# A two-layer hybrid diffusion step on one core: next layer's modulation loaded and multiplied inside the attention, and expert routing from first lists

## The chip, the cores and the metric

One NeuronCore of a Trainium2 chip runs the whole program in one launch. The metric is the device time of one execution in microseconds (us).

## The reference, cut to what matters

640 tokens (512 latent, 128 context) of width 1024 pass through two layers. All weights are float32.

```
mod  = silu(c) @ w_ada[l] + b_ada[l]          # 1024 -> 6 x 1024: shift1, scale1, gate1, shift2, scale2, gate2
h    = rms_norm(x) * (1 + scale1) + shift1
proj = h @ w_in                               # attention (8 heads, 2 kv heads), chunk MLP, convolution
x    = x + gate1 * (concat(rms_norm(attn), rms_norm(sgu), rms_norm(conv)) @ w_out)
h2   = rms_norm(x) * (1 + scale2) + shift2
group = argmax(h2 @ rg);  top-2 of the 4 experts of that group, by h2 @ re
x    = x + gate2 * sum over 2 experts of gate * ((silu(h2 @ w1) * (h2 @ w3)) @ w2)
```

The first third of `mod` (shift1, scale1) of layer 1 depends on `c` alone, so it can be computed at any time in layer 0. The experts see their tokens as blocks of 128 rows: each of 16 experts has one first block, and there may be further ones (up to 26 in all).

## The kernel before

Each engine runs its own program in order and waits on semaphores; nothing is scheduled at run time. TensorE (PE) gets float32 accuracy from pairs: ScalarE (ACT) copies a weight unit of 128x2048 (1 MB) from `raw` to `wH` in a rounded type, VectorE (DVE) writes the remainder to `wL`, and three matmuls use them. So a unit is free again in `raw` when DVE's half of the split is done.

Weights are loaded by the queue of SyncE (SP). `STREAM` lists the 1 MB units in order: `("w", l, n)` are units of `w_in` (n under 8) and `w_out` (8 to 11), `("ada", l, n)` those of `w_ada` (8 for each third `q` of the modulation), which PE reads straight from `raw` in `ada_mm`. Unit i goes to slot i mod 4 of `raw`, and SP waits before each load until the unit four places ahead of it has been used (`unit_used`). SP works through the list in order, so a load whose slot is free still stands behind one whose slot is not.

In the attention of a layer PE, DVE and ACT walk over steps u = 0 to 43 (five token tiles of eight heads, and four steps to drain). In step u PE computes the scores of head u, transposes the probabilities of step u-2, and every other step multiplies them with the values. DVE takes the row maximum (L1284), ACT the exponential (L880). Into the steps are woven: the 16 `ada` units of this layer (`ADA_AT`, steps 2 to 29), and from step 31 on the splits of units 8 and 9 in quarters of 128x512 (`QUARTER_AT`; `quarter_hi` on ACT, L744, `quarter_lo` on DVE, L1157). Then come the merged transposes, two halves of the output projection, h2 and the router.

Layer 1's first eight `ada` units stand at the end of layer 0's list: PE takes two between the halves of the projection and six among the router's steps (`ada_next`), and DVE adds the bias (`piece_add`) after the routing. In layer 0 the splits of the first expert's w1 and w3 (`m_split(0, 0)` and `m_split(1, 0)`) come after the routing too; in layer 1 they come on ACT among the copies of the router, and on DVE between `normalised(4)` and the routing.

The routing is a chain of small DVE operations over 128 partitions: ranks of the logits (twice: groups, then the experts of the chosen group), choice, counts by matmul, ranks of tokens within experts, a one-hot of these (`one_r`, L1420), and lists by ten matmuls (L1888); from them `idxs` (L1438), after which GpSimd (POOL) gathers rows of h2 for the first two blocks (L650). PE transposes them (L1898), ACT copies (`x_hi`, L979), DVE subtracts (`x_lo`, L1475), and `w13` starts (L1566 to L1568). `ctl` holds the number of blocks, `slot` the rows that tokens find their results in.

## Time and profile before

| | |
|---|---|
| runs, median (lowest to highest) | 1110.79 us (1108.39 to 1112.57), 3 runs |
| the profiled execution | 1111.54 us, of which the span is 1109.7 |
| busy share | PE 89%, DVE 60%, ACT 53%, POOL 22% |
| mean granted clock of TensorE | 0.951 |
| mean DMA rate | 224 GB/s; above 400 in the experts' stages |

### The profile page before, as it was taken

The numbers are of one execution on the slowest core, as the hardware profiler recorded it, in microseconds if no ns is written. First come the engines' busy times: TensorE is split into PE (matmuls) and PEld (weight loads), VectorE is DVE, ScalarE is ACT, GpSimd is POOL, SyncE is SP. The second block draws the span as 40 slices with busy tenths as digits, with TensorE's granted clock in tenths as the row PEclk, the third lists the DMA queues.
The fourth block names the chain that finished last, engine by engine and source line by source line (L and its number), as shares of the span: only waits on it lengthen the run. The fifth ranks groups of instructions, "written<-read, shape, count | busy, mean of one in ns | idle before, by whom it ended". The sixth has DMA issues, their size and how long they took to land.

```text
span 1109.7 us, 15792 instructions
## 1 busy us (share of the span) xinstructions
PE 987.5 (89%) x5588; PEld 759.7 (68%) x5588; DVE 668.7 (60%) x970; ACT 587.1 (53%) x929; POOL 247.5 (22%) x304
## 2 busy tenths in 40 slices
PE   4899989986998699998989999899789739999984
PEld 2688865765874588887757887467568637888861
DVE  0359125655276799988444831455625659999936
ACT  4452235655222598887267222565623418988822
POOL 3034015211131122230411500620203212222031
PEclk9899999999998799999999999899889959999998
DMA  9695227553156899996771321565313448999944
GB/s 319 235 276 205 76 62 273 194 183 130 34 214 249 333 387 401 417 401 260 297 209 40 111 79 39 200 242 200 115 57 133 150 167 329 408 417 411 366 154 173
DMA packets 89091, 248.16 MB, mean 224 GB/s; under 512 B 25773, under 2 KB 30381, under 8 KB 79817
## 3 DMA queue, kind: packets, MB, share of 16 engines
q1 hardware_dynamic: 75960, 209.54, 50.9%
q0 software_dynamic: 11632, 32.60, 8.5%
q10 hardware_dynamic: 1440, 5.24, 1.2%
q8 instruction: 36, 0.59, 0.2%
q14 instruction: 23, 0.18, 0.0%
HBM read 220.82 MB, written 30.21 MB: 226 GB/s over the span
## 4 chain that ended last, share of the span: by engine, by line
PE 68%; DVE 9%; DMA 9%; ACT 7%; issue 4%; SPq 1%; POOL 0%; ACTq 0%; DVEq 0%; POOLq 0%
PE ps L1559 12%; PE ps L1561 12%; PE ps L1560 12%; DMA pool<-in_moe_w 6%; PE ps L1566 4%; PE ps L1568 4%; PE ps L1567 4%; PE ps L1577 4%; PE ps L1749 3%; PE ps L1764 3%; PE ps L1959 2%; PE ps L1738 2%; DVE wL L1358 2%; ACT wH L938 2%; PE ps L1898 2%
## 5 line engine op out<-in xcount | busy, mean ns | idle before, releaser
L1559 PE MATMUL ps<-wH,actH 128*128 128x512 f32 x608 | 248.6, 409 | 10.0 <-DVE actL L1487 5.2
L1561 PE MATMUL ps<-wH,actL 128*128 128x512 f32 x608 | 240.9, 396 | 0.0
L1560 PE MATMUL ps<-wL,actH 128*128 128x512 f32 x608 | 240.1, 395 | 0.0
L1358 DVE TENSOR_TENSOR wL<-raw,wH 128x2048 fp32r<-128x2048 f32 x64 | 146.2, 2285 | 14.1 <-ACT wH L938 13.6
L1559 PEld LDWEIGHTS ps<-wH,actH 128*128 128x128 f32 x608 | 116.5, 192 | 38.4 <-issue 9.1
L1561 PEld LDWEIGHTS ps<-wH,actL 128*128 128x128 f32 x608 | 116.0, 191 | 26.0
L1560 PEld LDWEIGHTS ps<-wL,actH 128*128 128x128 f32 x608 | 116.7, 192 | 22.2
L938 ACT ACTIVATE wH<-raw 128x2048 fp32r<-128x2048 f32 x64 | 122.3, 1911 | 16.4 <-DMA raw<-in_moe_w 16.2
L1566 PE MATMUL ps<-wH,actH 128*128 128x512 f32 x256 | 105.2, 411 | 5.4 <-DVE wL L1358 2.8
L1568 PE MATMUL ps<-wH,actL 128*128 128x512 f32 x256 | 102.0, 398 | 0.0
L1567 PE MATMUL ps<-wL,actH 128*128 128x512 f32 x256 | 101.3, 396 | 0.0
L650 POOL DMA_INDIRECT pool<-h2s,idxc x28 | 51.1, 1824 | 196.5 <-PE ps L1898 157.8
L1284 DVE TENSOR_REDUCE nmax<-ps 128x1 f32<-128x640 f32 (+1 forms) x80 | 57.2, 716 | 61.9 <-PE ps L1739 61.9
L1358 DVE TENSOR_TENSOR wL<-pool,wH 128x2048 fp32r<-128x2048 f32 x32 | 73.2, 2286 | 15.1 <-ACT wH L938 15.1
L880 ACT ACTIVATE pool<-ps,nmax 128x640 f32<-128x640 f32 (+1 forms) x80 | 56.7, 708 | 45.9 <-DVE nmax L1284 45.3
L738 ACT ACTIVATE wH<-raw 128x2048 fp32r<-128x2048 f32 x19 | 36.4, 1938 | 53.7 <-PE ps L1561 37.9
L938 ACT ACTIVATE wH<-pool 128x2048 fp32r<-128x2048 f32 x32 | 61.2, 1912 | 3.9 <-DMA pool<-in_moe_w 3.9
L1749 PE MATMUL ps<-ident,pool 128*128 128x128 f32 x336 | 53.1, 283 | 9.4 <-DVE tabs L1292 4.7
L1566 PEld LDWEIGHTS ps<-wH,actH 128*128 128x128 f32 x256 | 49.1, 192 | 17.2 <-DVE wL L1358 4.0
L979 ACT ACTIVATE actH<-ps 128x512 fp32r<-128x512 f32 x64 | 38.3, 598 | 37.5 <-PE ps L1898 34.9
L1568 PEld LDWEIGHTS ps<-wH,actL 128*128 128x128 f32 x256 | 48.9, 191 | 11.2
L1567 PEld LDWEIGHTS ps<-wL,actH 128*128 128x128 f32 x256 | 49.1, 192 | 9.1
(261 smaller groups left out, 1662.6 us busy)
## 6 DMA issues: line engine op xcount, KB each, us to landing
raw<-in_moe_w SPq DMA_DIRECT2D x96, 512.0 KB, 8.6
raw<-in_w_ada SPq DMA_DIRECT2D x40, 1024.0 KB, 5.0
raw<-in_moe_w SPq DMA_DIRECT2D x16, 1024.0 KB, 12.6
pool<-in_moe_w SPq DMA_DIRECT2D x32, 512.0 KB, 7.8
pool<-in_moe_w SPq DMA_DIRECT2D x16, 1024.0 KB, 11.4
ys<-pool SPq DMA_DIRECT2D x32, 512.0 KB, 11.0
raw<-in_w_in SPq DMA_DIRECT2D x15, 1024.0 KB, 8.7
...
```

What stands on the lines that cost most here:

```text
L650: pl.indirect_dma_start(xg[:, parity, :], None, h2s[l], bass.IndirectOffsetOnAxis(idx[:, parity:parity + 1], 0), bounds_check=TOK - 1, oob ...
L880: act.activation(prob[:, u % 2, 0:keys], flat[:, 2 * N * (u % 2):2 * N * (u % 2) + keys], ACT.Exp, bias=nmax[:, u % 2:u % 2 + 1], accum_ou ...
L938: act.activation(wH[:, i if place is None else place, :], mraw[parity][i], ACT.Copy).then_inc(sem(f"m_hi{i}"), 1)
L1284: dve.tensor_reduce(nmax[:, u % 2:u % 2 + 1], flat[:, 2 * N * (u % 2):2 * N * (u % 2) + keys], X, ALU.max, negate=True).then_inc(sem("nmax ...
L1358: dve.tensor_tensor(wL[:, w, :], mraw[parity][i], f32(wH[:, w, :]), ALU.subtract).then_inc(sem(f"m_lo{i}"), 1)
L1559: pe.matmul(out, aH, wH[:, slot_, cols_], start=first, stop=False)
L1560: pe.matmul(out, aH, wL[:, slot_, cols_], start=False, stop=False)
L1561: return pe.matmul(out, aL, wH[:, slot_, cols_], start=False, stop=last)
L1566: pe.matmul(out, aH, hi, start=first, stop=False)
L1567: pe.matmul(out, aH, lo, start=False, stop=False)
L1568: return pe.matmul(out, aL, hi, start=False, stop=last)
L1749: m = pe.transpose(ps[:, 4 + c // 4, (c % 4) * P:(c % 4) * P + P], prob[:, w % 2, c * P:(c + 1) * P], ident[:, :])
```

## The change

- **Next modulation.** Layer 1's first eight `ada` units move in `STREAM` between units 8 to 11 of `w_out`, and PE multiplies one of them at the end of each of steps 33 to 40 of layer 0's attention (`NEXT_AT`), in bank 7. Unit 9's quarters move from steps 35 to 38 to 36 to 39 in layer 0 (`gap`). Bias loads and bias addition move ahead as well.
- **Splits.** Both layers split the first expert's w1 and w3 between `normalised(1)` and `normalised(2)`, and between `second_half(4)` and `normalised(4)`, on DVE.
- **Routing.** Ranks of groups and experts are taken at once, over 400 elements instead of twice 80. The lists of the 16 first blocks are made from token ranks that aren't reduced modulo 128 (a token beyond the 128th falls out of the one-hot). What only further blocks, gates and slots need comes after `idx_ready` (`more_rows`, `gate_logits`, `more_blocks`, `slots`), still ahead of the first `x_lo` on DVE; `more_idx` follows behind two `x_lo`.
- **Held reads.** SP waits for the second gather before it loads the third expert's w1 and w3, in both layers.
- **Identity transposes.** PE does 36 of them behind the list matmuls.

```diff
+WARM2 = 36
...
-    STREAM += [("w", _l, n) for n in range(int(_l == 0), 8)] + [("ada", _l, n) for n in range(8, 24)] + [("w", _l, n) for n in range(8, 12)]
-    if _l + 1 < DEPTH:
-        STREAM += [("ada", _l + 1, n) for n in range(8)]
+    STREAM += [("w", _l, n) for n in range(int(_l == 0), 8)] + [("ada", _l, n) for n in range(8, 24)]
+    NEXT = [("ada", _l + 1, n) for n in range(8 if _l + 1 < DEPTH else 0)]
+    STREAM += [("w", _l, 8)] + NEXT[0:3] + [("w", _l, 9)] + NEXT[3:6] + [("w", _l, 10)] + NEXT[6:8] + [("w", _l, 11)]
...
-        QUARTER_AT = {31 + i: (8 + i // 4, i % 4) for i in range(8)}
-
-        def ada_bank(l, q):
-
-            return 6 if l and q == 0 else 7
...
+        QUARTER_AT = [{31 + i + (gap if i >= 4 else 0): (8 + i // 4, i % 4) for i in range(8)} for gap in (1, 0)]
+
+        NEXT_AT = {NLT * NH + 1 + i: i for i in range(KD)}
...
                 load_w13(0, 1, None, 1)
                 sp.wait_ge(sem("h2"), at("h2", l, NT))
-                if l == 0:
-
-                    sp.wait_ge(sem("m_g0"), 16)
                 load_w13(1, 1, None, 1)
                 for p_ in range(2):
                     sp.wait_ge(sem(f"h2_stored{p_}"), at(f"h2_stored{p_}", l + 1, 0))
                 sp.wait_ge(sem("h2T_psum"), at("h2T_psum", l, NT))
                 load_w2(1, None, 1)
+
+                sp.wait_ge(sem("m_g1"), 16 if l == 0 else sp.snap(first * 8 + 16, min_val=16, max_val=16 * MAXB))
                 load_w13(0, 0, 1, 2)
                 load_w13(1, 0, 1, 2)
                 sp.wait_ge(sem("ctl_ready"), at("ctl_ready", l, 1))
...
+                if l + 1 < DEPTH:
+                    bias_in(l + 1, 0)
...
-                if l + 1 < DEPTH:
-                    bias_in(l + 1, 0)
...
+                next_gathers(0)
+                pl.wait_ge(sem("idx_ready"), at("idx_ready", l, 2))
+                with pl.Fori(1, h) as pair:
+                    next_gathers(pair)
...
                 h2_store(0)
+                w_read(act, l, 9)
+                m_split(0, 0, pairs)
                 mean_square(2, 1)
...
                 lT_out(0)
                 h2T_out(1)
+                w_read(act, l, 10)
+                m_split(1, 0, pairs)
                 lT_out(1)
...
-                if l + 1 == DEPTH:
-
-                    w_read(act, l, 9)
-                    m_split(0, 0, pairs)
...
-                if l + 1 == DEPTH:
-                    w_read(act, l, 10)
-                    m_split(1, 0, pairs)
...
-                if l + 1 < DEPTH:
-                    m_split(0, 0, pairs)
-                    m_split(1, 0, pairs)
...
                 m_split(0, 1, pairs)
+                act.wait_ge(sem("rt_late"), at("rt_late", l, 3))
                 silu(first, 0)
...
+                act.wait_ge(sem("ctl_ready"), at("ctl_ready", l, 1))
+                h = act.value_load(ctl[0:1, 0:1], min_val=MINB // 2 - 2, max_val=MAXB // 2 - 2) + 1
...
+                    if l + 1 < DEPTH and u == NT * NH + 1:
+                        piece_add(l + 1, 0)
...
                 second_half(2)
                 normalised(1)
+                m_split(0, 0, first)
                 normalised(2)
                 second_half(3)
                 normalised(3)
                 second_half(4)
+                m_split(1, 0, first)
                 normalised(4)
-                if l + 1 == DEPTH:
-                    m_split(0, 0, first)
-                    m_split(1, 0, first)
                 dve.wait_ge(sem("ss2"), at("ss2", l, 2 * NT))
...
-                def ranks(v):
-
-                    link(dve.tensor_tensor(diff, v.unsqueeze(2).to_broadcast([P, NT, 4, 4]), bc(v, 4), ALU.subtract))
-                    link(dve.tensor_tensor(diff, diff, mid(eps_, NT), ALU.is_gt))
-                    link(dve.reduce_sum(rank, diff, X))
-
-                ranks(gl)
-                link(dve.tensor_scalar(og, rank, 0.0, None, ALU.is_equal))
-                link(dve.tensor_tensor(pr, el.rearrange("p t (g e) -> p t g e", g=4), bc(og, 4), ALU.mult))
-                link(dve.reduce_sum(es, pr.rearrange("p t g e -> p t e g"), X))
-                ranks(es)
-                link(dve.tensor_scalar(sel, rank, 2.0, None, ALU.is_lt))
-                dve.tensor_tensor(Mb.rearrange("p t (g e) -> p t g e", g=4), bc(og, 4),
-                                  sel.unsqueeze(2).to_broadcast([P, NT, 4, 4]), ALU.mult).then_inc(sem("choice"), 1)
-
...
+                lgg = lg.rearrange("p t (g e) -> p (t g) e", e=4)
+                link(dve.tensor_tensor(diff, lgg.unsqueeze(2).to_broadcast([P, 5 * NT, 4, 4]), bc(lgg, 4), ALU.subtract))
+                link(dve.tensor_tensor(diff, diff, mid(eps_, 5 * NT), ALU.is_gt))
+                link(dve.reduce_sum(rank, diff, X))
+                rk = rank.rearrange("p (t g) e -> p t g e", g=5)
+                re = rk[:, :, 1:, :]
+                link(dve.tensor_scalar(og, rk[:, :, 0, :], 0.0, None, ALU.is_equal))
+                dve.scalar_tensor_tensor(out=Mb.rearrange("p t (g e) -> p t g e", g=4), in0=re, scalar=2.0, in1=bc(og, 4),
+                                         op0=ALU.is_lt, op1=ALU.mult).then_inc(sem("choice"), 1)
                 for c in range(2):
-                    link(dve.tensor_tensor(M[:, c].rearrange("p t (g e) -> p t g e", g=4), bc(og, 4),
-                                           o12[:, :, c, :].unsqueeze(2).to_broadcast([P, NT, 4, 4]), ALU.mult))
+                    link(dve.scalar_tensor_tensor(out=M[:, c].rearrange("p t (g e) -> p t g e", g=4), in0=re, scalar=float(c), in1=bc(og, 4),
+                                                  op0=ALU.is_equal, op1=ALU.mult))
                 M10 = M.rearrange("p c t e -> p (c t) e")
                 Mf = M.rearrange("p c t e -> p c (t e)")
                 pe10 = pr2.rearrange("p (c e) -> p c e", e=16)
+                link(dve.tensor_scalar(tl[:, :, 0, :], M10, tidx, None, ALU.mult))
+                link(dve.tensor_tensor(tl[:, :, 1, :], M10, bc(offs, NE), ALU.mult))
...
                 dve.wait_ge(sem("counts_psum"), at("counts_psum", l, 1))
+                link(dve.tensor_tensor(pr2.rearrange("p (c n) -> p c n", c=2), Mf, mid(ps[:, 5, 0:NT * 16], 2), ALU.mult))
+                link(dve.reduce_sum(q, pe10, X))
+                link(dve.tensor_copy(qb, q))
+
+                dve.tensor_tensor(one_r, bc(qb, P), mid(iota[:, :], 10), ALU.is_equal).then_inc(sem("lists"), 1)
 
                 link(dve.tensor_tensor(cmp4, bc(ps[:, 4, 0:16], 4), mid(thr, 16), ALU.is_gt))
...
+                def more_rows():
+
+                    link(dve.tensor_tensor(over, bc(q, 4), mid(thr, 10), ALU.is_ge))
+                    link(dve.reduce_sum(qd, over, X))
+                    link(dve.scalar_tensor_tensor(out=q, in0=qd, scalar=-128.0, in1=q, op0=ALU.mult, op1=ALU.add))
+                    link(dve.tensor_copy(qb, q))
+                    link(dve.tensor_tensor(one_r, bc(qb, P), mid(iota[:, :], 10), ALU.is_equal))
+
+                def gate_logits():
...
+                more_rows()
+                gate_logits()
+                more_blocks()
+                slots()
...
                 x_lo(0, first)
                 x_lo(1, first)
+                more_idx()
                 x_lo(0, first + 1)
...
+                    if l + 1 < DEPTH and u in NEXT_AT:
+                        if NEXT_AT[u] == 0:
+                            pe.wait_ge(sem("piece_done"), at("piece_done", l, 3))
+                        ada_mm(l + 1, NEXT_AT[u])
...
                 pe.wait_ge(sem("lists"), at("lists", l, 1))
                 for c in range(10):
-                    m = pe.matmul(ps[:, 0, 0:2 * LB], one_r[:, c, :], tl[:, c, :, :].rearrange("p s b -> p (s b)"), start=(c == 0), stop=(c == 9))
+                    m = pe.matmul(ps[:, 0, 0:2 * NE], one_r[:, c, :], tl[:, c, :, :].rearrange("p s b -> p (s b)"), start=(c == 0), stop=(c == 9))
                 m.then_inc(sem("list_psum"), 1)
+                for i in range(WARM2):
+                    pe.transpose(ps[:, 3, (i % 4) * P:(i % 4) * P + P], ident[:, :], ident[:, :])
+
+                def more_lists():
+
+                    pe.wait_ge(sem("lists"), at("lists", l, 2))
+                    for c in range(10):
+                        m = pe.matmul(ps[:, 5, 0:2 * (LB - NE)], one_r[:, c, :], tl2[:, c, :, :].rearrange("p s b -> p (s b)"), start=(c == 0), stop=(c == 9))
+                    m.then_inc(sem("list_psum"), 1)
 
...
-                pe.wait_ge(sem("ctl_ready"), at("ctl_ready", l, 1))
-                h = pe.value_load(ctl[0:1, 0:1], min_val=MINB // 2 - 2, max_val=MAXB // 2 - 2) + 1
+                pe.wait_ge(sem("idx_ready"), at("idx_ready", l, 1))
                 x_chunks(0, first, 0, pairs)
                 x_chunks(1, first, 0, pairs)
+                more_lists()
                 w13(0, first, 0)
                 x_chunks(0, first + 1, 1, pairs)
                 w13(1, first, 0)
                 x_chunks(1, first + 1, 1, pairs)
                 if l + 1 < DEPTH:
                     modc_cols(l + 1)
+                pe.wait_ge(sem("idx_ready"), at("idx_ready", l, 2))
+                pe.wait_ge(sem("ctl_ready"), at("ctl_ready", l, 1))
+                h = pe.value_load(ctl[0:1, 0:1], min_val=MINB // 2 - 2, max_val=MAXB // 2 - 2) + 1
```

On SP, at the end of layer 0's attention, before (`raw<-in_w_ada` behind the four `w_out` loads are layer 1's units; `quarter_lo` is DVE's split of units 8 and 9, `ada_read` a unit read by PE, `w_lo` the splits of units 10 and 11):

```order
L423 DMA raw<-in_w_ada 128x2048 [waits ada_read] x12
L430 DMA raw<-in_w_out 128x4x512 [waits ada_read] x4
L423 DMA raw<-in_w_ada 128x2048 [waits quarter_lo] x2
L423 DMA raw<-in_w_ada 128x2048 [waits w_lo] x2
L423 DMA raw<-in_w_ada 128x2048 [waits ada_read] x4
L448 DMA raw<-in_moe_w 128x1024 [waits ada_read]
```

And the same place of the changed kernel:

```order
L420 DMA raw<-in_w_ada 128x2048 [waits ada_read] x12
L427 DMA raw<-in_w_out 128x4x512 [waits ada_read]
L420 DMA raw<-in_w_ada 128x2048 [waits ada_read] x3
L427 DMA raw<-in_w_out 128x4x512 [waits quarter_lo]
L420 DMA raw<-in_w_ada 128x2048 [waits ada_read] x3
L427 DMA raw<-in_w_out 128x4x512 [waits quarter_lo]
L420 DMA raw<-in_w_ada 128x2048 [waits ada_read] x2
L427 DMA raw<-in_w_out 128x4x512 [waits ada_read]
L445 DMA raw<-in_moe_w 128x1024 [waits w_lo]
```

Three of the next layer's units now stand behind unit 9, and two behind unit 10; units 9 and 10 wait for DVE's splits of units 8 and 9.

On PE, step 39 of layer 0's attention and what follows, before (L1738 and L1739 are scores, L1749 transposes of probabilities, L1754 of an output, L1764 the product with the values):

```order
L1738 MATMUL ps<-actH,actL 128x512 [waits prob]
L1739 MATMUL ps<-actH,actL 128x512
L1738 MATMUL ps<-actH,actL 128x128
L1739 MATMUL ps<-actH,actL 128x128
L1749 MATMUL ps<-ident,pool 128x128 [waits pT,prob]
L1749 MATMUL ps<-ident,pool 128x128 x4
L1754 MATMUL ps<-ident,pool 128x128 [waits oT]
L1749 MATMUL ps<-ident,pool 128x128 [waits pT,prob]
L1749 MATMUL ps<-ident,pool 128x128 x4
L1764 MATMUL ps<-pool 64x128 [waits attn_done,pT]
L1764 MATMUL ps<-pool 64x128 x9
```

And in the changed kernel, from the transpose of the output on (L1584 is `ada_mm`, and `raw_loaded1` the landing of its unit in slot 1):

```order
L1761 MATMUL ps<-ident,pool 128x128 [waits oT]
L1584 MATMUL ps<-raw,cpad 32x512 [waits raw_loaded1]
L1584 MATMUL ps<-raw,cpad 32x512 x3
L1756 MATMUL ps<-ident,pool 128x128 [waits pT,prob]
L1756 MATMUL ps<-ident,pool 128x128 x4
L1771 MATMUL ps<-pool 64x128 [waits attn_done,pT]
L1771 MATMUL ps<-pool 64x128 x9
L1584 MATMUL ps<-raw,cpad 32x512 [waits raw_loaded2]
L1584 MATMUL ps<-raw,cpad 32x512 x3
L1756 MATMUL ps<-ident,pool 128x128 [waits pT,prob]
```

The last heads' transposes and products now stand behind the landing of units 6 and 7 of the next modulation.

On DVE, between the one-hot `one_r` and `idxs`, before:

```order
L1420 TENSOR_TENSOR pool<-pool,iota 128x1280 [waits dve_step]
L1421 TENSOR_TENSOR pool<-pool 128x160 [waits dve_step]
L1422 TENSOR_REDUCE pool<-pool 128x10 [waits dve_step]
L1423 TENSOR_TENSOR pool<-pool 128x10 [waits dve_step]
L1425 TENSOR_TENSOR pool<-pool 128x10 [waits dve_step]
L1426 TENSOR_SCALAR pool<-pool 128x10 [waits dve_step]
L1427 TENSOR_TENSOR pool<-pool 128x10x16 [waits dve_step]
L1428 TENSOR_TENSOR pool<-pool,pcon 128x10x10 [waits dve_step]
L1429 TENSOR_SCALAR pool<-pool,pcon 128x10x26 [waits dve_step]
L1430 TENSOR_TENSOR pool<-pool,pcon 128x10x26 [waits dve_step]
```

And now:

```order
L1403 TENSOR_TENSOR pool<-pool,iota 128x1280 [waits dve_step]
L1405 TENSOR_TENSOR pool<-ps,pcon 128x64
L1406 TENSOR_REDUCE pool<-pool 128x16 [waits dve_step]
L1407 SCALAR_TENSOR_TENSOR pool<-pcon,pool 128x16 [waits dve_step]
L1408 SCALAR_TENSOR_TENSOR pool<-pcon,pool 128x16 [waits dve_step]
L1411 COPY pool<-ps 128x16 [waits lists,list_psum,dve_step]
L1412 SCALAR_TENSOR_TENSOR idxs<-pool,ps 128x16 [waits dve_step]
```

Before, `lists` was signalled at L1430; now the one-hot itself signals it, and four small operations lie beside PE's list matmuls. The operations that vanished here stand after `idxs`.

## Rows read from the trace of the kernel before

**Rows 1.** The page's chain that ended last, by engine.

```profile
PE 68%; DVE 9%; DMA 9%; ACT 7%; issue 4%; SPq 1%; POOL 0%; ACTq 0%; DVEq 0%; POOLq 0%
```

**Rows 2.** Timeline of layer 0's attention end, PE: start us, duration, line, operation.

```profile
254.19 0.50 PE L1738 MATMUL ps<-actH,actL 128*128 128x512 f32 x1
...
260.61 0.50 PE L1738 MATMUL ps<-actH,actL 128*128 128x512 f32 x1
...
264.14 0.74 PE L1749 MATMUL ps<-ident,pool 128*128 128x128 f32 x5 [0.36 <-ACT pool L873]
...
267.74 1.31 PE L1764 MATMUL ps<-tabs,pool 128*64 128x128 f32 x20 [0.80 <-DVE pool L1255]
```

**Rows 3.** Timeline of the same stretch, DVE and ACT.

```profile
250.98 0.69 DVE L1157 TENSOR_TENSOR wL<-raw,wH 128x512 fp32r<-128x512 f32 x1 [0.74 <-ACT wH L744]
...
257.38 0.82 DVE L1284 TENSOR_REDUCE nmax<-ps 128x1 f32<-128x640 f32 x1
...
262.01 0.62 ACT L744 ACTIVATE wH<-raw 128x512 fp32r<-128x512 f32 x1
...
263.27 0.82 DVE L1284 TENSOR_REDUCE nmax<-ps 128x1 f32<-128x640 f32 x1
...
264.12 0.79 ACT L880 ACTIVATE pool<-ps,nmax 128x640 f32<-128x640 f32 x1
```

**Rows 4.** L423's 1 MB loads: one issued at 251.7, then four at 306.8 to 310.4.

```profile
DMA to landing us min/median/max: 4.8/4.8/4.8
...
DMA to landing us min/median/max: 6.4/7.6/10.3
```

**Rows 5.** Stretches: length, busy time of each engine, granted clock, DMA share, GB/s.

```profile
270.00:272.00 2.00, 0.55 (x3) 0.31 (x3) 0.29 (x2) 0.72 (x2) 0.80 (x3) 1.00 0.00 0
...
274.00:276.00 2.00, 0.95 (x3) 0.86 (x4) 0.99 (x2) 0.44 (x1) 0.00 (x0) 0.50 1.12 371
...
280.00:285.00 5.00, 5.00 (x26) 4.09 (x25) 1.01 (x2) 0.95 (x2) 0.00 (x0) 0.99 0.00 0
...
911.00:912.00 1.00, 1.00 (x4) 0.76 (x3) 0.00 (x0) 0.00 (x0) 0.00 (x0) 0.71 0.34 139
...
980.00:1000.00 20.00, 20.00 (x101) 16.76 (x100) 18.61 (x16) 17.62 (x19) 3.97 (x4) 1.00 1.03 421
```

**Rows 6.** Timeline of layer 0, ada matmuls in the projection, then h2 and routing.

```profile
308.45 1.92 PE L1577 MATMUL ps<-raw,cpad 128*32 128x512 f32 x16
...
343.67 1.28 DVE L1349 SCALAR_TENSOR_TENSOR pool<-x,stat,pool 128x1024 f32<-128x1024 f32 x1 [1.83 <-POOL stat L639]
...
350.15 0.26 DVE L1380 TENSOR_TENSOR pool<-ps,rb 128x100 f32<-128x100 f32 x1 [3.94 <-PE ps L1825]
...
361.63 0.18 DVE L1438 SCALAR_TENSOR_TENSOR idxs<-pool,ps 128x26 uint32<-128x26 f32 x1
...
371.02 1.28 DVE L1475 TENSOR_TENSOR actL<-ps,actH 128x512 fp32r<-128x512 f32 x2
```

**Rows 7.** Timeline of layer 1, h2, routing and the first expert matmul.

```profile
865.42 1.28 DVE L1349 SCALAR_TENSOR_TENSOR pool<-x,stat,pool 128x1024 f32<-128x1024 f32 x1 [0.45 <-POOL stat L639]
...
879.31 1.28 DVE L1349 SCALAR_TENSOR_TENSOR pool<-x,stat,pool 128x1024 f32<-128x1024 f32 x1 [3.38 <-POOL stat L639]
...
886.07 2.29 DVE L1358 TENSOR_TENSOR wL<-raw,wH 128x2048 fp32r<-128x2048 f32 x1 [2.00 <-ACT wH L938]
...
888.27 0.26 DVE L1380 TENSOR_TENSOR pool<-ps,rb 128x100 f32<-128x100 f32 x1
...
899.88 0.18 DVE L1438 SCALAR_TENSOR_TENSOR idxs<-pool,ps 128x26 uint32<-128x26 f32 x1
...
907.08 0.69 DVE L1475 TENSOR_TENSOR actL<-ps,actH 128x512 fp32r<-128x512 f32 x1 [3.15 <-ACT actH L979]
...
907.90 0.79 PE L1566 MATMUL ps<-wH,actH 128*128 128x512 f32 x1 [0.64 <-DVE actL L1475]
```

**Rows 8.** DVE groups of layer 1's routing: count, busy us, mean ns of one.

```profile
L1386 DVE TENSOR_TENSOR pool<-pool,pcon 128x80 f32<-128x80 f32 x2 | 0.5, 246 | 0.1
...
L1413 DVE TENSOR_TENSOR pool<-pool,ps 128x160 f32<-128x160 f32 x1 | 0.3, 320 | 0.0
...
L1420 DVE TENSOR_TENSOR pool<-pool,iota 128x1280 bf16<-128x1280 bf16 x1 | 1.5, 1491 | 0.0
```

More of the change, by code:

```diff
@@ L1433, in _ @@
-                link(dve.reduce_sum(own, pe10, X))
+                link(dve.tensor_tensor_scan(incl, ones_, more[:, 1:], 0.0, ALU.mult, ALU.add))
                 dve.wait_ge(sem("list_psum"), at("list_psum", l, 1))
                 dve.wait_ge(sem("lists"), at("lists", l, 1))
-                link(dve.tensor_copy(pr2[:, 0:LB], ps[:, 0, 0:LB]))
-                dve.scalar_tensor_tensor(out=idxs[:, :], in0=pr2[:, 0:LB], scalar=float(NOROW - 1), in1=ps[:, 0, LB:2 * LB],
+                link(dve.tensor_copy(pr2[:, 0:NE], ps[:, 0, 0:NE]))
@@ new lines, in slots @@
+                def slots():
+                    link(dve.tensor_tensor(pe10, M10, mid(bidx[:, 0:NE], 10), ALU.mult))
+                    link(dve.reduce_sum(own, pe10, X))
+                    link(dve.tensor_tensor(eb, eb, own, ALU.add))
+                    link(dve.tensor_tensor(own, own, over[:, :, 0], ALU.mult))
+                    link(dve.tensor_tensor(eb, eb, own, ALU.subtract))
+                    link(dve.scalar_tensor_tensor(out=qd, in0=eb, scalar=128.0, in1=q, op0=ALU.mult, op1=ALU.add))
+                    dve.tensor_copy(slot[:, :], qd).then_inc(sem("rt_late"), 1)
```

110 lines of the change are left out of this document (44 added, 66 removed).

## The prediction

> **What bounds the kernel now.** I read the page's chain of work first: PE holds 68% of it, DVE, DMA and ACT 7 to 9% each [rows 1], so the time is mostly matmul work, and between its stages there are short chains through other engines. The change touches two kinds of these. The reader should look at them in the timeline.
>
> The first is the end of layer 0's attention [rows 2, 3]. Scores of step 37 start at 254.19 and those of step 39 at 260.61, the last product with the values at 267.74; DVE takes the maximum of step 37 only at 257.38, some 2.3 us after its scores are done, because it has the quarters of units 8 and 9 to split. So PE has a little slack there, DVE and ACT none, and the DMA engines are nearly idle. A lone 1 MB load lands 4.8 us after its issue; the last of four issued within 3.6 us takes 10.3 [rows 4]. The granted clock is 1.00 until 272, 0.50 at 274 to 276 after PE had little to do, 0.99 again from 280 [rows 5].
>
> The second is the routing. It is one chain on DVE: in layer 0 from 350.15 to `idxs` at 361.81 (11.66 us), then the gather, then `x_lo` at 371.02 [rows 6]; in layer 1 from 888.27 to 900.06 (11.79), `x_lo` at 907.08, first expert matmul at 907.90 [rows 7]. After it the experts' blocks keep PE busy 20.00 of 20 us with the DMA share at 1.03 [rows 5]. What starts them earlier ends them earlier by the same: the loads follow the release of buffers, and shift along.
>
> **The change part by part: the next modulation in the attention.** Each unit is 0.95 us of PE (16 matmuls of two units take 1.92 [rows 6]). It removes 1.9 us of matmuls from the projection, and adds 7.6 to steps 33 to 40. What decides is when the units land. Slots 1 to 3 hold units 0 to 2 in good time. Unit 3 stands on SP behind unit 9 of `w_out`, which waits until DVE has split unit 8 in step 34: 250.98 + 0.69 = 251.67 [rows 3]. Two loads of 1 MB: 4.8 us for the first, 1.05 MB at 421 GB/s = 2.5 more for the second [rows 4, 5], so unit 3 lands at 259.0. PE, with two units' matmuls on it by then, wants it at about 255.2. It stands 3.8 us; the scores of step 37 come at 260.0 instead of 254.2, and of these 5.8 DVE's lag of 2.3 swallows a part: the maximum comes 3.5 us late. Units 4 and 5 land on PE's heels (261.5, 264.0) and cost 0.95 each, half hidden: 4.1 late at step 39.
>
> Unit 6 is worse. It stands on SP behind unit 10, which waits for the last quarter of unit 9, now in step 39, and that comes behind maximum, exponential and `quarter_hi` of the same step: 263.27, 264.12, + 0.79, + 0.62, + 0.69 [rows 3], with a copy of ACT ahead some 266.8; with 4.1 of delay 270.9. Again 7.3 us for two loads: 278.2. PE has nothing else to do from 268.2 on, since the last two heads' transposes stand behind the unit. It stands 10 us. Then unit 6 (0.95), what lay between 264.14 and 267.74 (3.6 [rows 2]), and unit 7 (0.95): the last product starts at 283.7, 16.0 us after 267.74.
>
> The clock adds to it: PE idles 4 and 10 us, more than the gap that took the clock down at 272 to 274 [rows 5], so the 5.5 us of PE work behind the second stand start at half speed, 2 us more, and 1 us behind the first. I take 19. Bounds: 13, if only the second stand counts and one 1 MB load less the first (4.8 and 2.5 being what they are, 10.5 us from scores to landing against about 1 us of other PE work), and 22, if the second load takes 1.6 us longer each time, as the last of the four does against my formula (4.8 + 3 x 2.5 - 3.6 = 8.7, measured 10.3 [rows 4]). Nothing behind gives this back: merging, projection and everything later wait for the last head.
>
> The Trainium skill ("DMA: Bandwidth & Descriptors", section "Anatomy of one DMA") says that DMA engines never wait on semaphores, since the wait is on the issuing sequencer ahead of dispatch; by this a load behind a waiting one isn't even known to the engines, which is what makes units 3 and 6 late. The same section's fit, 2.0 us + bytes at 436 GB/s, would make a pair 6.8 us instead of 7.3 (the lone load would be 4.4; the trace has 4.8), and the loss an estimated 1 us smaller.
>
> **Projection to routing.** The 1.9 us off PE in layer 0 is mostly lost: DVE and POOL lead there, and `normalised(4)` waits for a chain through ACT and POOL (idle 1.83 [rows 6]). The splits put in on DVE (2.29 each) fit into gaps in front of `normalised(2)` to (4) about to the limit. I walked both layers: layer 0 gains 0.75. In layer 1 the first split pushes `normalised(2)` from 865.42 (gap 0.45) by 1.8, which is caught up until `normalised(4)` at 879.31 (gap 3.38), where 0.2 is left as a gain. But ACT and DVE no longer have a split ahead of the last router copy and ahead of the routing (886.07 + 2.29, routing at 888.27 [rows 7], whereas layer 0 without it needs 6.5 from `normalised(4)` to the routing [rows 6], 8.96 in layer 1, so 2.5): 2.7 in all.
>
> **Routing to `idxs`.** Small operations cost 0.2 + 0.03 us between, 80 elements 0.246, 160 elements 0.320, so some 1 ns an element, and 400 elements about 0.58; the one-hot is 1.49 [rows 8]. Choice: 0.30 + 3 x 0.61 + 0.21 + 0.24 = 2.6 (before 3.2). To the one-hot's start: five operations beside the counts 1.25, then 0.35 + 0.35 + 0.2; one-hot 1.5: `lists` at 6.25 (before 10.6). Then 0.95 of small operations beside PE's lists, and 0.4: `idxs` after 7.5, so 4.2 earlier in layer 0 and 4.3 in layer 1.
>
> **`idxs` to the first expert matmul.** Here what was put off falls due: number of blocks 1.7, `more_rows` 2.4 with its second one-hot, `gate_logits` 1.5, `more_blocks` 2.0, `slots` 1.6, together 9.2 us on DVE ahead of `x_lo`. Before, `x_lo` came 9.2 after `idxs` in layer 0 (two splits stood there) and 7.0 in layer 1 (the gather). So layer 0 keeps its 4.2, layer 1 gives back 2.3 with the register load. The held reads cost nothing: the third expert's weights are wanted some 22 us after `idxs`, land 15 after, and DMA idles between. They make the gather quicker, but the gather isn't last any more.
>
> **Clock at the experts.** In layer 1 the first matmuls run at half clock from 907.90 until 911.5 (0.71 over 911 to 912 [rows 5]), 1.8 us lost, in layer 0 alike. The 36 transposes raise the clock; but they end at about `idxs` + 5.7, and PE then has 1 us of transposes and 0.5 of lists until `x_lo` ends at + 10. In the trace gaps of some 2 us took it down. Between 0 and 1.8 per layer; I take 0.95.
>
> **Sum.** + 19 (attention) - 0.75 - 4.2 - 0.95 (layer 0) - 2.7 - 4.3 + 2.3 - 0.95 (layer 1) = + 7.4 us. Against the profiled execution's own 1111.5 (span 1109.7) that is 1118.9; this execution lies 0.75 above the runs' median, so I forecast 1118.
>
> **The rivals.** First, that the units aren't late, the other side. It needs the loads' landings hidden: the point is where unit 6 lands within about 1 us of PE's wish. For it speaks that DMA is idle there and PE has slack; against it the two waits in SP's order. Then the attention costs 2 to 3 us (PE work in steps whose DVE part leads), and the result is - 11.6 + 3: 1102. A chance of 0.14.
>
> Second, the same late units, but cheaper, with no clock effect and the transposes paying in full: + 14.5 - 11.6 - 1.7 more from the clock = + 1.2, 1112, no measurable change. 0.2.
>
> Third, the routing doesn't do what it says for the time: DVE's 9.2 us grow (register load, copies of PSUM), or PE's lists stand behind the transposes, which at half clock would need 36 x 0.25 = 9 us. Then 3 us less come back: 1121. 0.12. The forecast itself has 0.54.
>
> **How the numbers follow.** The likeliest case gives 1118, with its bounds 1112 to 1123. The range, 1106 to 1123, takes in the second case and part of the third, and leaves out the first one's core and the upper tail. About 0.5% (5.6 us) is what a measurement of this kernel can tell from no change. Faster by more than that: the first rival, 0.15. Slower: the forecast's and the third's parts above 1116.4, 0.58. Within: 0.27.
>
> **What would show each step.** In the changed profile PE should stand some 4 us in front of the ada matmuls of step 36 and 10 us in front of those of step 39, with DMA as the releaser, and the last product of layer 0's attention start near 286. `idxs` should come 7.5 us after the routing's start in both layers, `x_lo` 9.2 to 9.5 after `idxs`, without idle time of DVE between. The routing of layer 1 should start 2.7 us earlier against its projection. The prediction is wrong if the attention of layer 0 ends less than 10 us later than before, or if the experts' stages (158 us from the first matmul to the last output) change their length by more than 3 us.

## The result and the profile after

The changed kernel takes 1123.4 us, median of 4 runs (1122.7 to 1125.0), against 1109.6 of before (1108.3 to 1112.6): ratio 1.0132, interval 1.0109 to 1.0156, so 13.8 us slower. 1118 was forecast, with a range up to 1123. The profiled executions (1122.7 of after, 1111.5 of before) differ by only 11.2 us.

Of the page, the busy shares hardly changed (PE 89%, DVE 60%, ACT 53%, POOL 22% before). The chain of work that ended last did: it has less PE and more DVE and POOL than before [rows 1].

```profile
PE 999.1 (89%) x5680; PEld 770.9 (69%) x5680; DVE 673.5 (60%) x966; ACT 587.0 (52%) x929; POOL 251.4 (22%) x304
...
PE 65%; DVE 12%; DMA 9%; ACT 7%; issue 4%; POOL 2%; SPq 0%; ACTq 0%; DVEq 0%; POOLq 0%
```

**End of layer 0's attention.** The timeline of the changed kernel; these rows answer to [rows 2, 3]. L427 is a load of `w_out`, L420 one of a modulation unit, L1584 the units' matmuls:

```profile
251.40 0.38 SPq L427 DMA_DIRECT2D raw<-in_w_out  x1
251.82 1.61 SPq L420 DMA_DIRECT2D raw<-in_w_ada  x3
...
256.41 0.63 ACT L744 ACTIVATE wH<-raw 128x512 fp32r<-128x512 f32 x1 [1.61 <-DMA raw<-in_w_out]
...
258.92 1.94 PE L1584 MATMUL ps<-raw,cpad 128*32 128x512 f32 x8 [4.09 <-DMA raw<-in_w_ada]
...
272.74 0.38 SPq L427 DMA_DIRECT2D raw<-in_w_out  x1
273.16 1.14 SPq L420 DMA_DIRECT2D raw<-in_w_ada  x2
...
280.43 1.93 PE L1584 MATMUL ps<-raw,cpad 128*32 128x512 f32 x8 [10.37 <-DMA raw<-in_w_ada]
...
287.86 1.31 PE L1771 MATMUL ps<-tabs,pool 128*64 128x128 f32 x20 [0.68 <-ACT tabs L873]
```

Unit 3 is issued right behind `w_out` 9 and PE stands 4.09 us for it, unit 6 behind `w_out` 10 and PE stands 10.37 us. Both then run at half clock (1.94 us for 8 matmuls; 1.06 at full). The last product starts at 287.86 instead of 267.74.

**Projection and routing of layer 0**, the same view (L1346 and L1348 are the two operations of `normalised`, L1355 DVE's split of an expert's weights; L633 is POOL's operation on one number a partition between ACT's square sums and `normalised`; L1376 the start of the routing, L1412 `idxs`, L1480 `x_lo`). They answer to [rows 6]:

```profile
346.74 1.22 DVE L1348 TENSOR_TENSOR pool<-pool 128x1024 f32<-128x1024 f32 x1
346.85 3.40 POOL L633 TENSOR_SCALAR stat<-stat 128x1 f32<-128x1 f32 x1 [2.68 <-ACT pool L917]
...
347.89 2.28 DVE L1355 TENSOR_TENSOR wL<-raw,wH 128x2048 fp32r<-128x2048 f32 x1
...
350.93 1.28 DVE L1346 SCALAR_TENSOR_TENSOR pool<-x,stat,pool 128x1024 f32<-128x1024 f32 x1 [0.76 <-POOL stat L634]
...
360.43 2.28 DVE L1355 TENSOR_TENSOR wL<-raw,wH 128x2048 fp32r<-128x2048 f32 x1
...
361.36 1.51 POOL L633 TENSOR_SCALAR stat<-stat 128x1 f32<-128x1 f32 x1 [4.76 <-ACT pool L917]
...
363.55 1.28 DVE L1346 SCALAR_TENSOR_TENSOR pool<-x,stat,pool 128x1024 f32<-128x1024 f32 x1 [0.84 <-POOL stat L634]
...
371.13 0.26 DVE L1376 TENSOR_TENSOR pool<-ps,rb 128x100 f32<-128x100 f32 x1 [5.03 <-PE ps L1833]
...
378.48 0.17 DVE L1412 SCALAR_TENSOR_TENSOR idxs<-pool,ps 128x16 uint32<-128x16 f32 x1
...
389.17 1.29 DVE L1480 TENSOR_TENSOR actL<-ps,actH 128x512 fp32r<-128x512 f32 x2 [1.18 <-issue]
...
395.94 0.69 DVE L1480 TENSOR_TENSOR actL<-ps,actH 128x512 fp32r<-128x512 f32 x1 [5.21 <-ACT actH L973]
```

The whole path by stages, from the starts of such rows, in us. "Half" is the first of the five DVE operations that take over the projection's first half (L1332 before, L1329 after); it starts 7.2 us ahead of `second_half(0)` in every profile. The expectations below call the same row the "first second half". `x_lo` is the first of its kind behind `idxs`. The four columns on the right are experiments 1, 7, 8 and 11 below, the second is experiment 12.

| stage | before | before again | after | modulation alone | splits moved | late work | all three |
|---|---|---|---|---|---|---|---|
| layer 0: start to half | 311.18 | 312.56 | 330.40 | 331.45 | 331.37 | 331.36 | 316.18 |
| half to routing | 38.97 | 38.97 | 40.73 | 36.76 | 37.90 | 40.74 | 37.44 |
| routing to `idxs` | 11.48 | 11.48 | 7.35 | 11.62 | 7.35 | 7.35 | 7.36 |
| `idxs` to `x_lo` | 9.39 | 9.39 | 10.69 | 8.54 | 10.69 | 6.94 | 7.31 |
| last output of layer 0 to half of layer 1 | 317.58 | 311.81 | 312.14 | 314.30 | 313.55 | 311.12 | 313.50 |
| layer 1: half to routing | 40.91 | 41.55 | 40.66 | 40.87 | 37.44 | 40.74 | 37.43 |
| routing to `idxs` | 11.61 | 11.61 | 7.36 | 11.61 | 7.35 | 7.35 | 7.36 |
| `idxs` to `x_lo` | 7.20 | 7.33 | 10.39 | 7.25 | 10.38 | 7.07 | 6.94 |

### The profile page after: what moved, and what is told of

Same layout as the page of the kernel before. It is cut to its first block, busy times and chain, and to the rows that moved or that the text cites. A ratio compares the mean times of both kernels' runs of the same rounds, so it can differ in the third digit from the quotient of the medians.

```text
span 1120.9 us, 15967 instructions
## 1 busy us (share of the span) xinstructions
PE 999.1 (89%) x5680; PEld 770.9 (69%) x5680; DVE 673.5 (60%) x966; ACT 587.0 (52%) x929; POOL 251.4 (22%) x304
## 4 chain that ended last, share of the span: by engine, by line
PE 65%; DVE 12%; DMA 9%; ACT 7%; issue 4%; POOL 2%; SPq 0%; ACTq 0%; DVEq 0%; POOLq 0%
PE ps L1566 10%; PE ps L1568 10%; PE ps L1567 10%; PE ps L1584 4%; PE ps L1573 4%; PE ps L1575 4%; PE ps L1574 4%; PE ps L1756 3%; PE ps L1771 3%; DMA raw<-in_moe_w 3%; DMA pool<-in_moe_w 3%; PE ps L1745 2%; PE ps L1974 2%; DVE wL L1355 2%; PE ps L1746 2%
## 5 line engine op out<-in xcount | busy, mean ns | idle before, releaser
L1355 DVE TENSOR_TENSOR wL<-raw,wH 128x2048 fp32r<-128x2048 f32 x64 | 146.2, 2285 | 12.3 <-ACT wH L938 12.3
L1568 PEld LDWEIGHTS ps<-wH,actL 128*128 128x128 f32 x608 | 115.4, 190 | 25.6
L1567 PEld LDWEIGHTS ps<-wL,actH 128*128 128x128 f32 x608 | 115.9, 191 | 22.0
L938 ACT ACTIVATE wH<-raw 128x2048 fp32r<-128x2048 f32 x64 | 122.4, 1912 | 11.8 <-PE ps L1568 6.3
L645 POOL DMA_INDIRECT pool<-h2s,idxc x28 | 47.0, 1680 | 203.9 <-PE ps L1910 179.1
L1355 DVE TENSOR_TENSOR wL<-pool,wH 128x2048 fp32r<-128x2048 f32 x32 | 73.1, 2285 | 14.6 <-ACT wH L938 14.6
L1584 PE MATMUL ps<-raw,cpad 128*32 128x512 f32 x320 | 48.5, 682 | 15.2 <-DMA raw<-in_w_ada 14.5
L1745 PEld LDWEIGHTS ps<-actH,actL 128*128 128x128 f32 x144 | 28.1, 195 | 43.6 <-issue 33.2
## 6 DMA issues: line engine op xcount, KB each, us to landing
pool<-in_moe_w SPq DMA_DIRECT2D x16, 1024.0 KB, 10.5
ys<-pool SPq DMA_DIRECT2D x32, 512.0 KB, 10.8
```

The costliest lines, as they stand in the source:

```text
L938: act.activation(wH[:, i if place is None else place, :], mraw[parity][i], ACT.Copy).then_inc(sem(f"m_hi{i}"), 1)
L1355: dve.tensor_tensor(wL[:, w, :], mraw[parity][i], f32(wH[:, w, :]), ALU.subtract).then_inc(sem(f"m_lo{i}"), 1)
L1567: pe.matmul(out, aH, wL[:, slot_, cols_], start=False, stop=False)
L1568: return pe.matmul(out, aL, wH[:, slot_, cols_], start=False, stop=last)
L1584: m = pe.matmul(ps[32 * j:32 * j + 32, 7, :], c32, raw[:, POS["ada", l, n] % RAWS, j * N:(j + 1) * N], start=(kt % group == 0), stop=(kt % ...
```

## The experiments

Eleven kernels, each with 4 to 12 runs, and one more profile of the kernel before. Ratios are to the kernel before, with their 95% interval. A difference between two kernels is the difference of their ratios times 1109.6 us; with these intervals it is good to some 4 us, so the traces decide where the time went.

**1. The modulation part alone** on the kernel before: the order of units, `NEXT_AT`, the gap in `QUARTER_AT`, `bias_in` and `piece_add` moved, `ada_next` emptied.

> The kernel before with the modulation part alone: units loaded among the units of w_out, eight units' matmuls in steps 33 to 40 of layer 0's attention, piece_add in step 33's place, nothing in the projection or routing; routing, held reads, splits and transposes as before. Theory A (the cost sits in layer 0's attention and is local): last product of layer 0's attention +20 us against 267.74, PE standing 4 us in front of one unit and 10 us in front of another, as in the changed kernel; and by the changed kernel's trace, where the granted clock is 0.50 over 364 to 370 once no units fill PE between the router's matmuls, another +1 us from normalised(4) to the routing of layer 0 (6.5 before). Total about +19, some 1129. Theory B (the modulation costs only what shows net, and the new routing loses): total +5 or less. The clock's luck in layer 1's attention is +-3 us.

1128.4 us, ratio 1.0178 (1.0158 to 1.0198): 19.8 us. The stands are there again:

```profile
260.15 1.94 PE L1578 MATMUL ps<-raw,cpad 128*32 128x512 f32 x8 [4.25 <-DMA raw<-in_w_ada]
...
281.64 1.93 PE L1578 MATMUL ps<-raw,cpad 128*32 128x512 f32 x8 [10.45 <-DMA raw<-in_w_ada]
...
288.98 1.31 PE L1765 MATMUL ps<-tabs,pool 128*64 128x128 f32 x20 [0.68 <-ACT tabs L873]
```

Theory A holds, but for its last part: `normalised(4)` to the routing is 6.35 us here, not 7.5, at clock 1.00, though no units fill PE. So the rest of the change gives back only 1.0178 - 1.0132, 5 us, where 10.8 were forecast (- 4.2 - 0.95 - 2.7 - 4.3 + 2.3 - 0.95).

**2, 3. `w_out` 9, or 9 and 10, from another queue** in the changed kernel.

```
+                    if kind == "w" and l + 1 < DEPTH and n in (9, 10):
+                        continue            # on SP
+                w_out_load(9)               # on POOL, ahead of rest_stats(3); 10 behind attn_stats(3)
```

> The changed kernel with layer 0's unit 9 of w_out loaded from GpSimd's queue instead of SP's, so that units 3 to 5 do not stand behind its wait. Unit 10 stays on SP, and unit 6 behind it. Theory A (order of waits on SP makes the units late, each stand on its own): the first stand of 4.1 us goes, the second one of 10 us stays, and PE works through steps 36 to 38 up to 4 us earlier; since unit 10 then also comes up to 4 us earlier, the last product comes at 284 instead of 287.9: 4 us faster, 1119.5. Rival: the loads are late because of the DMA engines' rate, not the order: no change, 1123.

> The changed kernel with units 9 and 10 of w_out both loaded from GpSimd's queue in layer 0, so that no unit of the next modulation stands behind a wait of w_out's splits on SP. Theory A: no stand over 1 us in front of a unit; the last product of layer 0's attention at 270 to 272 instead of 287.9 (before: 267.74, plus PE work of 7.6 us of which DVE's lead hides the most); 16 us faster than the changed kernel, about 1107, and 3 us faster than before. Rival (PE's 7.6 us of matmuls are not hidden): last product at 276, 1112.

1.0195 (1.017 to 1.0221) and 1.0142 (1.0123 to 1.016): slower than the changed kernel, and the same. The last product starts at 291.50 and 284.85, where 284 and 270 to 272 were expected. Neither theory is enough. The timeline with unit 9 alone moved, then with both:

```profile
251.33 0.78 POOL L607 DMA_DIRECT2D raw<-in_w_out  x1 [3.06 <-DVE wL L1166]
...
263.18 0.63 ACT L758 ACTIVATE wH<-raw 128x512 fp32r<-128x512 f32 x1 [8.71 <-DMA raw<-in_w_out]
...
284.58 1.94 PE L1598 MATMUL ps<-raw,cpad 128*32 128x512 f32 x8 [10.58 <-DMA raw<-in_w_ada]
```

```profile
253.43 0.78 POOL L607 DMA_DIRECT2D raw<-in_w_out  x1 [3.06 <-DVE wL L1168]
...
268.13 0.63 ACT L760 ACTIVATE wH<-raw 128x512 fp32r<-128x512 f32 x1 [11.56 <-DMA raw<-in_w_out]
```

The units now ran free on SP, and `w_out` 9 landed 11.8 and 14.7 us after its issue instead of 5.0. Units that SP issued up to 4.2 us after it landed first. The first wait moved from PE to ACT; with unit 10 still on SP, the second stayed on PE (10.58 us). It is not GpSimd's queue as such: `w_out` 10, issued there at 282.20 in the second run with little else under way, landed 5.5 us later. Two things add up. First, six small loads of bias and modulation, issued on the same queue from 245 to 248 us, landed only at 252.6 to 258.3 in the run with unit 9 alone. Second, the engines were full and shared between the queues: over 256 to 262 us in that run, SP's queue (q1) and GpSimd's (q0) moved nearly the same (packets, MB, share of the 16 engines):

```profile
q1 hardware_dynamic: 184, 1.25, 52.5%
q0 software_dynamic: 272, 1.04, 44.5%
```

The Trainium skill ("DMA: Bandwidth & Descriptors", section "Issuing engines are not separate DMA queues") says that transfers from all issuing engines run on the same 16 DMA engines and interleave. These two lines agree.

**4. The order alone**, on SP, same slots:

```
+                units = list(range(START[l], START[l + 1]))
+                if l + 1 < DEPTH:
+                    e = START[l + 1]
+                    units[-8:] = [e - 7, e - 8, e - 6, e - 5, e - 3, e - 2, e - 4, e - 1]
```

> The changed kernel with the same slots and the same queue (SP), but in layer 0 units are issued in the order 3, w_out 9, 4, 5, 6, 7, w_out 10, w_out 11 instead of w_out 9, 3, 4, 5, w_out 10, 6, 7, w_out 11. The runs with w_out 9 on GpSimd's queue showed that it then lands 11 to 14 us after its issue, among loads that had overtaken it, and ACT waited for it: order and rate of the DMA engines act together. Here w_out 9 has only unit 3 ahead, which is issued 4 us before it. Theory A (units are late through SP's order): unit 3 in time, w_out 9 lands at 256.5 as before, units 4 to 7 each 0 to 2 us late; last product of layer 0's attention at 272 to 275 instead of 287.9; 14 us faster than the changed kernel: 1109. Rival (five 1 MB loads in 15 us can't be had at some 420 GB/s without a stand, whatever their order): last product at 282 or later, 1118.

1110.4 us, 1.0017 (0.9996 to 1.0038), 12.8 us off the changed kernel. The rival falls: the last product is back at 274.54, as theory A said, and ACT, not PE, has the longest wait left. It waits for `w_out` 9, which now lands 7.2 us after its issue, not 5 as expected:

```profile
251.60 0.38 SPq L431 DMA_DIRECT2D raw<-in_w_out  x1
252.02 10.77 SPq L424 DMA_DIRECT2D raw<-in_w_ada  x4
...
258.82 0.63 ACT L748 ACTIVATE wH<-raw 128x512 fp32r<-128x512 f32 x1 [3.82 <-DMA raw<-in_w_out]
...
261.33 1.06 PE L1588 MATMUL ps<-raw,cpad 128*32 128x512 f32 x8 [0.40 <-DMA raw<-in_w_ada]
...
274.54 1.31 PE L1775 MATMUL ps<-tabs,pool 128*64 128x128 f32 x20 [0.68 <-ACT tabs L877]
```

**5. The same order with the modulation part alone.**

> The kernel before with the modulation part alone (as the first experiment, 1.0178), and the units issued in the order 3, w_out 9, 4, 5, 6, 7, w_out 10, w_out 11. If the order takes 12.8 us off here too: ratio 1.0063, 7 us slower than before: then the eight units' matmuls in the attention cost some 7 us in their steps even when the loads are nearly in time (ACT waits 3.8 us for w_out 9, PE's 7.6 us of matmuls), and 2 us of it come back in the projection. If it comes out at before or under it, the order was the whole loss.

1.0021 (1.0003 to 1.0039): 2 us slower than before, so the order takes 17 of the modulation's 20 us by the ratios. The traces show 13.2 of them up to half (331.45 to 318.27); 3.5 more lie in the unchanged stretch to layer 1 (314.30 to 310.78), which differs between profiles anyway (experiment 12). Half still comes 6 to 7 us later than in both profiles of before. Of that 2.2 return before the routing (36.72 us) and 0.9 ahead of `x_lo` (8.53): there DVE no longer has `piece_add` (0.68 us) between the two splits, nor a wait of 0.3 ahead of the first.

**6. Transposes where units stood between the router's matmuls** (8, 16, 8).

> The changed kernel with transposes of the identity (result unread, 8, 16 and 8 of them) where the units of the next modulation stood between the router's matmuls, in both layers. Theory C (without the units the granted clock falls to 0.50 ahead of the routing): the clock stays at 1.00 from 360 to 371, and normalised(4) to the routing takes 6.5 us in both layers instead of 7.5: 2 us faster than the changed kernel, 1121.5. Rival (the time goes to ACT's copies, which got m_split ahead of them): no change in that distance.

1.0182 (1.0158 to 1.0205), slower than the changed kernel. `normalised(4)` to the routing is 7.86 us in layer 0 and 6.77 in layer 1 (7.58 and 7.46 in the changed kernel). In layer 0 the first eight transposes end at 359.8, PE then stands 2.0 us, and the granted clock falls to 0.50 at 362.5 all the same; it is 1.00 again from 366. In layer 1 it stays at 1.00. So theory C explains 0.7 us of layer 1 and nothing in layer 0. Why the whole is 5 us slower was not followed up.

**7. DVE's splits moved.**

```
-                m_split(0, 0, first)
                 normalised(2)
                 second_half(3)
+                m_split(0, 0, first)
                 normalised(3)
                 second_half(4)
-                m_split(1, 0, first)
                 normalised(4)
+                m_split(1, 0, first)
```

> The changed kernel with DVE's two splits of the projection's end moved: the first from between normalised(1) and normalised(2) to between second_half(3) and normalised(3), the second from ahead of normalised(4) to behind it. Theory P (second_half(t), ACT's square, POOL's power, normalised(t) are one serial chain a tile, so a split ahead of second_half(3) costs its whole 2.3 to 2.5 us, while the idle time behind second_half is cover): first second half to routing 37.3 us instead of 40.73 in layer 0 (36.76 without splits) and 37.8 instead of 40.66 in layer 1; 6 us faster than the changed kernel, 1117. Rival Q (the routing's start is late through ACT's splits and the clock of 0.50 in the router): normalised(4) comes 2.5 us earlier but the routing less than 1 us earlier; 1121.5 or more.

1118.0 us, 1.0082 (1.0055 to 1.011): 5.5 us off. Half to routing is 37.90 and 37.44 us (37.3 and 37.8 expected), 2.8 and 3.2 less, where rival Q allowed less than 1: it falls. Of these, 2.1 us in each layer lie ahead of `normalised(4)`, in the chain that theory P names. The other 0.7 and 1.1 lie behind it, where the clock plays a part: it is 0.50 for 3.4 us instead of 6.8 in layer 0, and 1.00 throughout in layer 1. POOL's row beside the split, once in its new place and once with no split near:

```profile
353.60 2.28 DVE L1355 TENSOR_TENSOR wL<-raw,wH 128x2048 fp32r<-128x2048 f32 x1
...
354.54 1.51 POOL L633 TENSOR_SCALAR stat<-stat 128x1 f32<-128x1 f32 x1 [4.76 <-ACT pool L917]
...
356.73 1.28 DVE L1346 SCALAR_TENSOR_TENSOR pool<-x,stat,pool 128x1024 f32<-128x1024 f32 x1 [0.85 <-POOL stat L634]
...
361.45 0.30 POOL L633 TENSOR_SCALAR stat<-stat 128x1 f32<-128x1 f32 x1 [4.76 <-ACT pool L917]
```

**8. Late work behind `x_lo`.**

```
                 more_rows()
-                gate_logits()
                 more_blocks()
-                slots()
...
-                dve.wait_ge(sem("ctl_ready"), at("ctl_ready", l, 1))
-                h = dve.value_load(ctl[0:1, 0:1], ...) + 1
...
                 x_lo(0, first)
                 x_lo(1, first)
+                gate_logits()
+                slots()
                 more_idx()
+                dve.wait_ge(sem("ctl_ready"), at("ctl_ready", l, 1))
+                h = dve.value_load(ctl[0:1, 0:1], ...) + 1
                 x_lo(0, first + 1)
```

> The changed kernel with gate_logits, slots and the load of the block count's register put behind the first two x_lo on DVE (3.1 us of small operations and 1.2 us in which nothing runs), more_rows and more_blocks left in front. Theory R (the work put off stands in front of the first expert matmul on DVE): idxs to x_lo falls from 10.7 and 10.4 us to about 7.3, where the gather's row in layer 1 of before stands (7.2), and the third x_lo stays where PE's first four chunks put it: 3 us a layer, 6 in all, 1117. Rival (what is put behind is missed by ACT's silu or the third x_lo): third x_lo or hidden later, no change, 1123.

1112.8 us, 1.0027 (1.0008 to 1.0046): 11.6 us off, twice what was expected. `x_lo` comes 6.94 and 7.07 us after `idxs`, released by ACT's copy of the gathered rows and no longer by DVE itself:

```profile
379.45 0.17 DVE L1412 SCALAR_TENSOR_TENSOR idxs<-pool,ps 128x16 uint32<-128x16 f32 x1
...
386.39 1.29 DVE L1478 TENSOR_TENSOR actL<-ps,actH 128x512 fp32r<-128x512 f32 x2 [0.52 <-ACT actH L973]
...
392.02 0.69 DVE L1478 TENSOR_TENSOR actL<-ps,actH 128x512 fp32r<-128x512 f32 x1 [0.78 <-ACT actH L973]
```

The third `x_lo` is 12.57 us behind `idxs` (17.46 in the changed kernel), in layer 1 12.52 (16.92): 9.3 us in both layers together, where the first `x_lo` gained 7.1. These 2.2 us more are the clock. (The other 2.3 of the 11.6 are within the intervals.) The windows of the changed kernel, then of this one (busy us of PE, PEld, DVE, ACT, POOL, then the granted clock, DMA share, GB/s):

```profile
385.00:388.00 3.00, 0.54 (x12) 0.32 (x10) 2.61 (x13) 0.81 (x2) 1.21 (x2) 0.84 0.27 75
388.00:391.00 3.00, 1.09 (x3) 0.89 (x4) 1.53 (x4) 0.00 (x0) 0.00 (x0) 0.50 0.87 274
391.00:394.00 3.00, 3.00 (x9) 2.34 (x8) 0.00 (x0) 0.00 (x0) 0.00 (x0) 0.52 0.94 326
```

```profile
384.00:387.00 3.00, 1.41 (x19) 1.30 (x18) 2.27 (x8) 1.08 (x2) 0.25 (x1) 1.00 0.34 116
387.00:390.00 3.00, 2.86 (x13) 2.39 (x14) 2.73 (x13) 0.00 (x0) 1.21 (x2) 1.00 0.63 150
390.00:393.00 3.00, 3.00 (x17) 2.54 (x16) 1.70 (x7) 2.32 (x2) 0.00 (x0) 1.00 0.95 258
```

In the changed kernel PE runs into the stand ahead of `x_lo` at full clock and comes out at half.

**9. The same, without the change's 36 transposes.**

> The changed kernel with gate_logits, slots and the register load behind the first two x_lo, as before, and the 36 transposes of the change taken out. With them, this order gained 11.6 us where 6 were forecast, and the granted clock was 1.00 at the first expert matmuls. Theory T (the transposes pay only once the wait behind them is short): without them the first expert matmuls run at 0.50 again, the third x_lo comes 6.7 us after the first instead of 5.5, 1.2 to 1.8 us a layer: 1112.8 + 3 = 1116. Rival (the clock was up by chance, or the transposes do nothing): 1112.8, no change.

1.006 (1.0038 to 1.0082), 3.7 us more than with them; the intervals overlap. The trace is plainer: the clock is 0.50 over 387 to 390, the third `x_lo` 14.02 and 13.13 us after `idxs`, 1.45 and 0.6 later than with the transposes (of it 0.3 in each layer already at the first `x_lo`). They pay here.

**10. More transposes in front of the first expert matmul**, in the changed kernel.

> The changed kernel with 2 x 30 more transposes of the identity (result unread) in PE's idle stretch between the first x_chunks and the first expert matmul, on both sides of more_lists, in both layers. Theory C2 (the 36 transposes of the change raise the clock, but a stand of PE of some 5 us in front of the first expert matmul takes it down again, 0.50 over 388 to 391 and 0.52 over 391 to 394 in the changed kernel): the clock stays at 1.00 until 400, the third x_lo comes 5.0 us after the first instead of 6.7, 1.7 us a layer, 3.4 in all, 1120. Rival: transposes end late and push the first expert matmul by what they save, no change.

1.0145 (1.0114 to 1.0177), no gain. The clock stays at 1.00, but the transposes end later than `x_lo`: the first expert matmul starts at 392.12, where the two `x_lo` of 389.57 would have let it start near 390.3. The rival holds.

**11. The three edits that helped, together** (4, 7 and 8).

> The changed kernel with the three edits that helped alone: the units' order of issue (12.8 us less by the ratios), DVE's two splits moved (5.5 less), gate_logits, slots and the register load behind the first two x_lo (11.6 less). If the three are independent: 1123.4 - 29.9 = 1093.5, 15 us faster than before. If they share a cause (the clock, or the rate of the expert loads that a faster start runs into): 1100 or more. In the trace: last product of layer 0 near 275, first second half to routing 38, idxs to x_lo 7.

1094.8 us (1089.3 to 1097.6), 0.9866 (0.984 to 0.9892): 15 us faster than before, and 29.5 off the changed kernel by the ratios, where the three alone add up to 29.9. So they are independent as far as this can be told.

**12. The kernel before again.**

> The kernel before, unchanged, for a second profile. From the last output of layer 0's experts to the first second half of layer 1 its first profile took 317.6 us; the changed kernel and all experiments took 310.6 to 314.3 there, in code that is the same. If this is chance (where the granted clock falls to 0.50 in that stretch): the second profile lies at 311 to 315 too. If the change itself makes that stretch faster: 317 again.

1109.2 us, and 311.81 us for the stretch in question: its 317.58 in the first profile was chance.

## Why the prediction fell short

Direction and main mechanism were right; the time is 0.4 us above the range, 5.4 above the forecast. Of 9.25 us of misses in the traces, 4.95 lie between projection and routing, 2.2 in a register load and 1.9 in the clock at the experts. Point by point:

- **Attention of layer 0**, forecast + 19: half is 19.2 later in the changed kernel (17.8 against the second profile of before), the stands 4.1 and 10.4 us (3.8 and 10 foreseen), the last product at 287.9 (286). A pair of loads took 7.5 and 7.7 us from the first's issue (7.3 used). The estimate of 6.8 by the Trainium skill ("DMA: Bandwidth & Descriptors", section "Anatomy of one DMA") is further off; the section gives its fit for one DMA issued from GpSimd, and these are two from SP. The whole modulation part measured 19.8 by the ratio against 18.25 forecast.
- **Projection to routing, the step that failed**, forecast - 0.75 in layer 0 and - 2.7 in layer 1. Measured + 1.76 (38.97 to 40.73) and - 0.25. "The splits put in on DVE fit into gaps in front of `normalised(2)` to (4) about to the limit" and "is caught up until `normalised(4)`" were wrong. Each tile is a serial chain: `second_half`, ACT's square sum, POOL's two operations, `normalised`. DVE's idle time ahead of `normalised(3)` lies behind `second_half(3)`; a split ahead of that only moves the chain. And POOL got nothing done beside such work: its 0.30 us operation took 3.40 (346.85 to 350.25), over the second operation of `normalised(1)` and up to the end of the split at 350.17, and 1.51 at the second split. Without splits layer 0 takes 36.76 (experiment 1). So taking the units' matmuls off PE there was worth 2.2, not "mostly lost", and the splits cost 4.0 in layer 0 (2.8 ahead of `normalised(4)`, 1.2 behind it, at the lower clock). Moving DVE's two splits brought 5.5 us, both layers together.
- **Routing to `idxs`**, 7.5 us to the end of `idxs`: 7.52 and 7.53 (start to start 7.35 in the table). Right.
- **`idxs` to the first expert matmul**, forecast 9.2 to 9.5 from the end of `idxs`: 10.52 and 10.22 (10.69 and 10.39 from its start in the table). The 9.2 us of work were right (the last of `slots` ends at 387.98, 9.5 after `idxs` starts); the register load on DVE behind them had a few tenths at most in the forecast and cost 1.18 and 0.94 us in which nothing runs. That this work stood on the path was foreseen; that a third of it and this load, put behind `x_lo`, are worth 9 us in the traces (11.6 by the ratios) was not.
- **Clock at the experts**, forecast - 0.95 a layer: none. The third `x_lo` came 6.77 and 6.53 us after the first (6.75 and 6.67 before), since PE stood again behind the transposes and the clock was 0.50 when the experts began. In experiment 8 against 9 the transposes are worth 0.6 to 1.45 a layer.
- **Experts' stages**: first `x_lo` to last output 158.3 and 158.8 us against 158.8 and 158.7 before (158.4 and 160.7 in its second profile). As assumed. So nothing speaks against the held reads, which no experiment tested by themselves.

Put together from the traces, the misses are + 0.2, + 2.5 and + 2.45, + 1.3 and + 0.9, + 1.9 (clock): 9.25 on the forecast of 7.4, which is 16.7. The profiled before had 5.4 us more in an unchanged stretch (317.58 against 312.14), which leaves 11.2, the difference of the two executions; that it comes out to the tenth is luck, since smaller differences cancel. The medians' 13.8 lies between.

Of the rivals, the third was nearest in time (1121) and right in a part: the register load did add to DVE's work, 2.2 us of the rival's 3 in both layers together. PE's lists did not stand behind the transposes, and no rival had the 5 us between projection and routing. The first (units in time) is experiment 4's kernel: 1110.4, not 1102, since the routing part gave 5 us and not 10.8, and the last product is still 6.8 us later than before, not 2 to 3.
